# Hybrid attention and mixture-of-experts block on one core: one projection run per NSA step, attention a step deeper, maxima and copies ahead of the normalisation

## What is computed

```python
h = rms_norm(x, ln1[l]); proj = h @ w_in[l]          # 5688 columns
o_a = diff_attention(...)                            # 4 heads: softmax(s1) - lam * softmax(s2)
o_b = forgetting_attention(...)                      # 8 heads with decay c[q] - c[k]
o_c = nsa_attention(...)                             # 16 heads in 4 groups:
    # gate0 * compressed + gate1 * selected + gate2 * window attention, softmax each
x = x + concatenate([o_a, o_b, o_c]) @ w_out[l]
x = x + hier_moe(rms_norm(x, ln2[l]), ...)           # 64 experts, top 2 of one group
return rms_norm(x, ln_f)
```

## Time and profile before

| | |
|---|---|
| median of 3 runs | 2164.24 us (2161.39 to 2165.48) |
| the profiled execution | 2159.91 us, span 2157.8 us |
| PE busy | 1828.8 us, 85% of the span |
| DVE, ACT, POOL busy | 640.3, 477.3, 461.4 us (30%, 22%, 21%) |
| mean granted clock of PE | 0.944 of full speed |

### The profile page before, as it was taken

One profiled execution on the slowest core, in us unless ns is written; L12 is line 12 of the kernel. 1 busy time (PEld: TensorE's weight loads), 2 busy tenths in 40 slices (PEclk: granted clock), 3 DMA queues, 4 the chain that ended last, 5 costly groups with the idle time before them and its releaser, 6 DMA issues. The chain is left out here.

```text
span 2157.8 us, 27745 instructions
## 1 busy us (share of the span) xinstructions
PE 1828.8 (85%) x11130; PEld 1282.2 (59%) x11130; DVE 640.3 (30%) x1275; ACT 477.3 (22%) x1005; POOL 461.4 (21%) x340
## 2 busy tenths in 40 slices
PE   6999999999999987999839888888878888888881
PEld 4887777776666654788725545455545555555540
DVE  4423344436656677100221111111111111111115
ACT  4222333224344343222301101010010101010101
POOL 2323333232112120344031111111111111111110
PEclk9999999999999997999959999999999999999996
DMA  9452233232122130133549999999999999999985
GB/s 269 121 160 69 76 79 78 59 79 69 40 60 53 46 118 1 59 98 103 208 156 379 424 427 427 424 426 425 427 426 424 423 424 425 425 423 421 424 364 236
DMA packets 190374, 527.21 MB, mean 244 GB/s; under 512 B 65938, under 2 KB 149170, under 8 KB 162394
## 3 DMA queue, kind: packets, MB, share of 16 engines
q1 hardware_dynamic: 171498, 509.15, 61.3%
q0 software_dynamic: 18800, 17.00, 2.3%
HBM read 530.38 MB, written 46.03 MB: 267 GB/s over the span
## 5 line engine op out<-in xcount | busy, mean ns | idle before, releaser
L790 PE MATMUL PJ<-ht_rounded,ring_rounded 128*128 128x512 f32 (+1 forms) x928 | 322.5, 401 | 4.5 <-ACT at_region L1149 3.8
L1032 PE MATMUL PJ<-at_region,ring_region 128*64 128x256 f32 x1024 | 260.3, 419 | 68.9 <-DMA at_region<-in_w_up 67.9
L1032 PE MATMUL PJ<-ht_region,ring_region 128*64 128x256 f32 x1024 | 238.0, 393 | 44.2 <-DMA ht_region<-in_w_up 44.2
L1033 PE MATMUL PJ<-at_region,ring_region 128*64 128x256 f32 x1024 | 261.0, 420 | 0.0
L1032 PEld LDWEIGHTS PJ<-at_region,ring_region 128*64 128x64 f32 x1024 | 152.7, 152 | 158.4 <-issue 102.8
L1033 PE MATMUL PJ<-ht_region,ring_region 128*64 128x256 f32 x1024 | 238.7, 394 | 0.0
L728 POOL DMA_INDIRECT y_scratch<-ring_region,s_idx x64 | 64.5, 1008 | 779.2 <-DVE ring_region L1659 753.5
L1032 PEld LDWEIGHTS PJ<-ht_region,ring_region 128*64 128x64 f32 x1024 | 142.9, 142 | 122.6 <-issue 72.6
L676 POOL TENSOR_TENSOR ring_rounded<-ring_region,at_rounded 128x2048 fp32r<-128x2048 f32 (+1 forms) x31 | 139.7, 4505 | 343.3 <-ACT at_rounded L1094 343.3
L676 POOL TENSOR_TENSOR ring_rounded<-ring_region,ring_rounded 128x2048 fp32r<-128x2048 f32 x30 | 137.8, 4592 | 323.1 <-ACT ring_rounded L1094 323.1
L1651 DVE TENSOR_TENSOR ring_region<-ring_region,PJ 64x256 f32<-64x256 f32 x64 | 27.1, 423 | 593.1 <-ACT ring_region L1295 593.1
(11 more groups left out here) (244 smaller groups left out, 2626.6 us busy)
## 6 DMA issues: line engine op xcount, KB each, us to landing
at_region<-in_w_gate SPq DMA_DIRECT2D x32, 2048.0 KB, 14.4
at_region<-in_w_up SPq DMA_DIRECT2D x32, 2048.0 KB, 21.6
at_region<-in_w_down SPq DMA_DIRECT2D x32, 2048.0 KB, 21.5
ht_region<-in_w_gate SPq DMA_DIRECT2D x32, 2048.0 KB, 15.0
ht_region<-in_w_up SPq DMA_DIRECT2D x32, 2048.0 KB, 22.7
x_region<-in_w_down SPq DMA_DIRECT2D x32, 2048.0 KB, 22.5
ring_region<-in_w_in SPq DMA_DIRECT2D x36, 1024.0 KB, 5.9
ring_region<-in_w_out SPq DMA_DIRECT2D x16, 1024.0 KB, 5.1
```

Of the source, the lines that this page charges most:

```text
L790: ins = mm(out, w[:, k, 0:width], h[:, k, :], start=k == 0 and i == 0, stop=k == KT - 1 and i == 2)
L1032: mm(GU[0:CAP, 0:D_EXPERT], x, gate[:, j, :], start=j == 0, stop=j == KT - 1)
L1033: ins = mm(GU[CAP:2 * CAP, 0:D_EXPERT], x, up[:, j, :], start=j == 0, stop=j == KT - 1)
```

## The change

1. `LOOK` is 3. The scores of three steps are issued ahead of the loop, and fillings start and end a step earlier. S still has two halves.
2. `fillings()`: a unit of 4 steps keeps two places in each step; a unit of 20 has one place in each step (`fill(n, 1)` is empty there). The first unit has only step 0 for the tiles of the second: v in `fill(0, 0)`, then the turn, q and k together in `fill(0, 1)`.
3. The loops: PE does `values` of the step before ahead of `transpose_probs`, and `scores` last. ACT does the fillings first and `exps(n + 2)` behind `copy_pT`. DVE does `row_max(n + 2)` ahead of `copy_pT(n)`, and `normalise(n + 1)` last.
4. `row_max`: one `tensor_tensor_reduce` for each head adds the bias and takes the reduction of the nearest (up to) 256 keys; a `tensor_reduce` goes ahead of it over the farther keys, if there are any, and gives its starting value. Queries and bias are stored negated so that a minimum does for the negated maximum. Fox keeps its three or four instructions.
5. `normalise`: the product `coef` is gone; `tensor_scalar` multiplies by both values. 
6. `split_tile` and `split_mix`: four instructions of 128x512 for one of 128x2048.

```diff
-LOOK = 2
+LOOK = 3
+SIGN = {"diff": -1.0, "fox": 1.0, "nsa": -1.0, "cmp": -1.0, "slc": -1.0, "win": -1.0}
...
-        slots = [(n, half) for n in range(lo, hi) for half in range(2)]
-        slots = slots[:-1] if len(slots) > 4 else slots
+        slots = [(n, half) for n in range(lo, hi) for half in range(2 if len(STEPS[HEADS[g][0]]) == NT else 1)]
+        if len(slots) < 4:
+            (n, half), last = slots[0], slots[-1]
+            for i in range(FIRST[g + 1], FIRST[g + 2]):
+                out[n][half].append((i, 0, KT, False))
+                n, half = last
+                if COLUMNS[i][1] == "v":
+                    out[n][half].append((i, KT, KT, True))
+            continue
+        slots = slots[:-1]
...
-                nc.gpsimd.tensor_tensor(w_low[n % RING][:, :, 0:width], ring[n % RING][:, :, 0:width],
-                                        w_high[n % 2][:, :, 0:width].bitcast(F32), ALU.subtract).then_inc(w_split, 1)
+                for k in range(0, KT, 4):
+                    ks = slice(k, k + 4)
+                    ins = nc.gpsimd.tensor_tensor(w_low[n % RING][:, ks, 0:width], ring[n % RING][:, ks, 0:width],
+                                                  w_high[n % 2][:, ks, 0:width].bitcast(F32), ALU.subtract)
+                ins.then_inc(w_split, 1)
...
                 fill(n, 0)
+                if n >= 1:
+                    values(n - 1)
                 transpose_probs(n)
+                fill(n, 1)
                 if n + LOOK < ALL_STEPS:
                     scores(n + LOOK)
-                fill(n, 1)
-                values(n)
+            values(ALL_STEPS - 1)
...
             exps(0)
+            exps(1)
             for n in range(ALL_STEPS):
-                if n + 1 < ALL_STEPS:
-                    exps(n + 1)
+                after_fill(n, 0)
                 if n >= 1:
                     out_copy(n - 1)
-                after_fill(n, 0)
                 copy_pT(n)
+                if n + 2 < ALL_STEPS:
+                    exps(n + 2)
                 after_fill(n, 1)
...
-                    link(v.tensor_tensor(sc, sc, b, ALU.add))
-                v.tensor_reduce(nmx[:, par, :], S[:, par, :, 0:W], AX_X, ALU.max, negate=True).then_inc(max_ready, 1)
+                near = min(W, 2 * P)
+                if near < W:
+                    link(v.tensor_reduce(far_min[:, par, :], S[:, par, :, 0:W - near], AX_X, ALU.min))
+                for half in range(2):
...
+                    ins = v.tensor_tensor_reduce(sc, sc, b, 1.0, far_min[:, par, half:half + 1] if near < W else -NEG,
+                                                 ALU.add, ALU.min, nmx[:, par, half:half + 1])
+                ins.then_inc(max_ready, 1)
...
-                        link(v.tensor_tensor(coef[:, par, :], gates[:, qb, which:which + 2], c, ALU.mult))
...
+                            ins = v.tensor_scalar(p, p, c[:, half:half + 1], gates[:, qb, which + half:which + half + 1],
+                                                  ALU.mult, ALU.mult)
...
             for n in range(ALL_STEPS):
                 after_fill(n, 0)
+                if n + 2 < ALL_STEPS:
+                    row_max(n + 2)
                 copy_pT(n)
                 if n + 1 < ALL_STEPS:
                     normalise(n + 1)
-                if n + LOOK < ALL_STEPS:
-                    row_max(n + LOOK)
```

More of the change, by code:

```diff
@@ L1140, in take_out @@
                 else:
-                    ins = fn(q_live[g % 2][name == "q1"], unit0.get(n, PJ[:]), ACT.Copy, scale=SCALE)
+                    ins = fn(q_live[g % 2][name == "q1"], unit0.get(n, PJ[:]), ACT.Copy, scale=SIGN[kind] * SCALE)
                 ins.then_inc(staged_a, 1)
@@ L1155, in _ @@
             act.wait_ge(strip_ready, 1)
-            fn(strip_sb[0:T5_HEADS, :], Oflat[0:T5_HEADS, 0:STRIP], ACT.Copy).then_inc(strip_copied, 1)
+            fn(strip_sb[0:T5_HEADS, :], Oflat[0:T5_HEADS, 0:STRIP], ACT.Copy, scale=-1.0).then_inc(strip_copied, 1)
             def copy_kv(j):
@@ L1201, in exps @@
                     ins = fn(probs[:, par, 0, 0:P].rearrange("p (h n) -> p h n", h=2), S[:, par, :, 0:2 * CMP_PAD],
-                             ACT.Exp)
+                             ACT.Exp, scale=-1.0)
                 else:
@@ L1205, in exps @@
                         ins = fn(probs[:, par, half, 0:(qb + 1) * P], S[:, par, half, 0:(qb + 1) * P], ACT.Exp,
-                                 bias=nmx[:, par, half:half + 1], accum_out=rsum[:, par, half:half + 1])
+                                 bias=nmx[:, par, half:half + 1], scale=SIGN[kind], accum_out=rsum[:, par, half:half + 1])
                 ins.then_inc(exp_done, 1)
@@ L1459, in row_max @@
                     link(v.tensor_tensor(sc, sc, bcast(diag, 1, 2), ALU.add))
[L1460 to L1466, removed]
-                    link(v.tensor_tensor(sc, sc, b, ALU.add))
-                v.tensor_reduce(nmx[:, par, :], S[:, par, :, 0:W], AX_X, ALU.max, negate=True).then_inc(max_ready, 1)
+                    v.tensor_reduce(nmx[:, par, :], S[:, par, :, 0:W], AX_X, ALU.max, negate=True).then_inc(max_ready, 1)
+                    return
+                near = min(W, 2 * P)
+                if near < W:
+                    link(v.tensor_reduce(far_min[:, par, :], S[:, par, :, 0:W - near], AX_X, ALU.min))
+                for half in range(2):
+                    sc = S[:, par, half, W - near:W]
+                    b = bias[0][:, u, 2 * P - near:2 * P] if kind == "diff" else \
+                        bias[(u + 1) % 2][:, 2 * pr + half, 2 * P - near:2 * P]
+                    ins = v.tensor_tensor_reduce(sc, sc, b, 1.0, far_min[:, par, half:half + 1] if near < W else -NEG,
+                                                 ALU.add, ALU.min, nmx[:, par, half:half + 1])
+                ins.then_inc(max_ready, 1)
             def normalise(n):
@@ L1484, in normalise @@
                     link(v.reciprocal(rinv[:, par, :], rsum[:, par, :]))
-                    link(v.tensor_tensor(coef[:, par, 0:1], neglam, rinv[:, par, 1:2], ALU.mult))
-                    link(v.tensor_scalar(p2, p2, coef[:, par, 0:1], None, ALU.mult))
+                    link(v.tensor_scalar(p2, p2, rinv[:, par, 1:2], neglam, ALU.mult, ALU.mult))
                     ins = v.scalar_tensor_tensor(p1, p1, rinv[:, par, 0:1], p2, ALU.mult, ALU.add)
@@ L1490, in normalise @@
                     link(v.reciprocal(c, rsum[:, par, :]))
-                    if kind != "fox":
-                        which = NSA_HEADS * (1 if kind == "slc" else 2) + u * 4 + pr * 2
-                        link(v.tensor_tensor(coef[:, par, :], gates[:, qb, which:which + 2], c, ALU.mult))
-                        c = coef[:, par, :]
-                    v.tensor_scalar(p1, p1, c[:, 0:1], None, ALU.mult)
-                    ins = v.tensor_scalar(p2, p2, c[:, 1:2], None, ALU.mult)
+                    which = NSA_HEADS * (1 if kind == "slc" else 2) + u * 4 + pr * 2
+                    for half, p in enumerate((p1, p2)):
+                        if kind == "fox":
+                            ins = v.tensor_scalar(p, p, c[:, half:half + 1], None, ALU.mult)
+                        else:
+                            ins = v.tensor_scalar(p, p, c[:, half:half + 1], gates[:, qb, which + half:which + half + 1],
+                                                  ALU.mult, ALU.mult)
                 ins.then_inc(normed, 1)
@@ L1518, in after_fill @@
                         take_out(tile)
-            for n in range(LOOK):
-                row_max(n)
+            row_max(0)
+            row_max(1)
             normalise(0)
```

12 lines of the change are left out of this document (7 added, 5 removed).

## The result

The changed kernel took 2142.93 us (median of 4 runs, 2139.95 to 2144.50), the kernel before on the same chip 2164.86 (4 runs, 2161.39 to 2168.47): a ratio of 0.9904, with its interval 0.9887 to 0.9920. It is faster by 21.9 us. I had forecast 2121, a gain of twice that (43); 2142.9 lies in the range, near its slow end. The profiled execution took 2142.35 us with a span of 2140.30, so the two profiled spans differ by 17.5 us.

What follows compares the result with a forecast made beforehand. PE's work bounds the diff, fox and filled NSA stages; in the unfilled steps engines wait for each other. -5.3 - 15 - 6.9 + 5.9 - 22 = -43.3 from 2159.9 gives 2116.6, plus 4.3 for the median: 2121 us, range 2106 to 2145.

Steps and rivals of the forecast that it cites:

- Runs, 5.3 us: Filled NSA steps: 18 instead of 34 projection runs per unit, each costing 0.11 us beyond its matmuls; 5.3 us less.
- Waits in the filled NSA steps, 15 us: Filled NSA steps: projections cover PE's waits, chiefly values for ACT's copy; 15 of 16.7 us idle time gone.
- Diff and fox units, 6.9 us: Diff and fox units: projections now cover the wait of values for ACT's copy; 6.9 us less.
- The start, 5.9 us: Start of the loop: new PE waits before the third scores, q and k; 5.9 us more.
- The unfilled steps, 22 us: Last 22 steps, without projections: shorter waits between engines and less DVE work take the stage from 87 to 65 us.
- DVE nearly solid: Expected sign in the last steps: DVE busy almost without gaps, with no wait of normalise for ACT.
- The fused pair, put at 0.6 us: row_max: two fused instructions over 256 columns take 0.6 us together, so the exchange gains and costs zero.
- The collisions, 2 us back in the last stage: Unfilled steps: DVE's tensor_scalar still meets POOL's smaller pieces, for three tiles; 2 us added back (bounds 0 and 7).
- The waits of the filled stages come back: Rival, filled NSA steps: ACT's fillings delay copy_pT, so only the runs are saved there; 2136 us, chance 0.11.
- My own test: Filled NSA steps: the forecast would be wrong if PE still waited over 10 us for ACT.
- the low clock: Rival, last steps: PE's clock stays low, so the stage takes some 76 us instead of 65; 2132 us, chance 0.12.
- Slow fusion: Rival, row_max: the fused pair takes 2.0 us instead of 0.6, so the kernel ends slower; 2207 us, chance 0.04.

Runs made afterwards that it cites:

- E4: The changed kernel with two places for projections again in each NSA step, as before the change: 2147.60 us.
- E2: The changed kernel with long NSA units using all 20 places for projections, so the last place is no longer empty: 2124.49 us.
- E3: The changed kernel with DVE doing row_max(n + 2) ahead of after_fill(n, 0), places unchanged: 2127.34 us.
- E6: The changed kernel with scores of step 2 behind the first projections and, in step 0, the turned v copied before the exponentials of step 2: 2134.55 us.
- E5: The changed kernel with the old row_max and its signs, one sum and one reduction over all keys: 2146.69 us.
- E1: The changed kernel with POOL's split_tile and split_mix as one instruction per tile again: 2154.23 us.

## Why the prediction was right and wrong

Up to step 89 the forecast had -5.3 - 15 - 6.9 + 5.9 = -21.3 us; measured were +7.0, a miss of 28.3. PE's idle time was to fall by 16.0 and fell by 0.7: 15.3 us of the miss. The rest is nearly all clock. After, the granted clock (0.98 on average, before 1.00) is at its lower level for 27 us in this part, before for 3; at half speed the difference costs up to 12 us, and the forecast had no such term. Against the miss stand 0.7 us that the unfilled steps gained beyond the forecast and 1.8 gained behind them. And of the 4.3 us by which I set the median above the profiled execution, only 0.6 were there. That last 3.7 us made the forecast look nearer than it was.

**Runs, 5.3 us:** right. From step 32 to 89 the profile has 96 runs before and 50 after, and in both the second matmul of a run starts 0.34 us behind the first, 0.11 more than the others: 4.9 us. From step 52 to 67, all at the full clock, the time went from 67.40 to 64.08: 1.2 us for 11 runs fewer, and 2.3 less idle time. E4's 4.7 mixes several effects.

**Waits in the filled NSA steps, 15 us: this step failed.** Its mechanism held, its account did not. The waits of `values` for ACT's copy vanished, as argued. But I wrote that what is moved or added on DVE "is hidden by PE's projections, with 98 us of room over 60 steps, 1.6 a step". That is an average. DVE's queue is short of time just once per unit, where it first waits for k's projection and then has `row_max` ahead of `normalise`, and there PE has no projection at all. The order of the program showed both: the last place is empty, and `row_max(n + 2)` was moved to stand behind `after_fill(n, 0)`. The waits that took the place cost 12.6 us. Behind them the clock was at its lower level, 1.2 GHz, for 17 us in all, which costs up to 8.5 us, where the stage before had up to 1.7; a clock that falls in the filled stages was put at nothing. E2 and E3 give back 18.4 and 15.6 us; E2, at 2124.5, comes within 4 us of the forecast.

**Diff and fox units, 6.9 us:** right. From step 4 to 16 each unit is 1.54 us shorter, and from 16 to 24 each about 1.2: 6.9 us over these five. `values` no longer waits there. The waits of a projection for the turned tile, 7.6 us before, stayed, as forecast. After, from 163 to 502 us:

```profile
PE PJ L805 <- ACT at_region L1166: 9.7, 8, 2.9
PE PJ L819 <- ACT at_region L1149: 2.2, 7, 0.6
```

One wait of 2.9 us and one of 0.6 belong to the start. Without them 6.8 us are left for the turned tile, 2.9 of them in one wait at 461.7 us, and there are 1.6 new ones in which the turn waits for v's copy.

**The start, 5.9 us:** right in the waits, nearly one by one. Forecast were 2.8 for the third scores, 3.6 less what was there ahead of q, 0.9 for k. Measured: 2.5, 0.6 and 2.9, and 0.7, together 6.7 us where the kernel before waited 1.5, so 5.2 more. At the 2.9 us wait the granted clock fell too, which costs up to 1.7 more; in E6, where 1.6 us of that wait are left, it did not fall there.

**The unfilled steps, 22 us:** right, 87 to 65 us. Of PE's two leading waits there, 13.3 us for `normalise` and 8.8 for the copy, 6.4 and 3.0 are left, and DVE now waits 10.2 us for PE's transposes. The waits of the last stage, after:

```profile
DVE at_region L1524 <- PE PT L903: 10.2, 10, 2.0
...
PE PT L899 <- DVE at_region L1503: 3.4, 2, 1.7
PE O L924 <- ACT at_region L1230: 3.0, 4, 1.0
PE PT L903 <- DVE at_region L1516: 3.0, 4, 1.2
```

DVE was busy 51.9 us, not the floor of 58 that I had summed, so the 65 came from latency and not from DVE being full. My "DVE nearly solid" was wrong, and with it a part of the reasoning behind a right number; that it came out to the microsecond is luck.

**The fused pair, put at 0.6 us:** 0.41 us from one to the next for 256 columns (685.64 to 686.05 above), with the accumulator's read beside it. The exchange that I put at zero gains a few microseconds at most (E5).

**The collisions, 2 us back in the last stage:** in the wrong place, and undersized as a whole. I priced the split only in the last stage, though POOL meets DVE in every unit; E1 gives it 11.3 us, and none of them in the last stage.

**The rivals.** "The waits of the filled stages come back" foresaw the size, 2136, and missed the engine: it named ACT, it was DVE. My own test, that PE would wait over 10 us for ACT, would have let this pass; the right test names the idle time of the stage, whatever its owner. The stage of the last steps had a clock of 0.87, where it had been 0.79, so the low clock there did not decide; it fell at six places ahead of them that I had not looked at, three of them the ends of the units. Slow fusion is out.

## What to carry to other kernels

When a schedule moves work onto an engine that is "hidden", look at the places where the cover is missing, not at the average room: list the empty places of the plan, and at each follow the queue of the engine that is waited for next. An engine that waits for a late producer should have everything that doesn't need this producer ahead of it in its queue. And judge a removed wait by the idle time of the whole stage after the change: here the wait's name changed and the sum stayed.

## What the hardware showed that I had not expected

A gap of PE can cost more than itself: 4.2 us of waiting at step 68 was followed by granted clocks of 0.53 and 0.62 over the next two stretches of 4 us, and transposes that take 1.09 us for eight in E3 took 1.94. The cost varies: behind the like wait at step 48 the lower clock lasted half as long. Taking 10 us of idle time away gave 14.8 up to step 89 (E2). In E3 a stretch with PE busy 2.88 of 4 us was followed by one at 1.00.

Splitting a POOL instruction helps DVE, but not by the ratio of the sizes. Two `tensor_scalar` in succession took 2.97 us instead of 1.00 beside four pieces of 1.3 us. DVE met one piece, and then the next: they took 1.57 and 1.48 us, and each ended 0.28 us behind the end of a piece, as the one of 4.80 ended 0.28 behind POOL's in E1. Still the longest single `tensor_scalar` of L1516 fell from 4803 ns (E1) to 1571. The Trainium skill (SBUF — State Buffer, SBUF: two separate sides) states an exclusive lock that is held for the full instruction, the other engine fully blocked. The traces agree with it (4.80 beside 4.49 us, and at most 1.09 us beyond the usual time beside a piece of 1.26), and show besides that the second DVE instruction was held up anew.

The fused sum and minimum over 256 columns, one operand in PSUM and one in SBUF, takes 0.49 us and starts 0.41 us apart; a plain sum of that width takes 0.43. The Trainium skill (Vector Engine (DVE) Microarchitecture Reference, Points that are easy to get wrong) states half the rate for a three-operand instruction with two non-bf16 SBUF sources; no run here has that case with an accumulator. Without one the kernel before has it: its L1487, with two float32 sources in SBUF, takes 0.750 us for 128x512, and L1454, with one source in PSUM, 0.751, so no halving was seen there. The prediction's "no row shows it" overlooked these.
